# Two transformer blocks on one core: the first norm split by kinds of token, and keys and values moved ahead of the second half of the modulation

## What is computed

```python
def rmsnorm(x, g):
    xf = x.astype(jnp.float32)
    y = xf * lax.rsqrt(jnp.mean(xf * xf, axis=-1, keepdims=True) + EPS)
    return (y * g.astype(jnp.float32)).astype(x.dtype)

def adaln(cvec, w_mod, b_mod):
    m = jax.nn.silu(cvec) @ w_mod + b_mod
    return jnp.split(m, 6, axis=-1)

def modulate(x, g, shift, scale):
    return rmsnorm(x, g) * (1 + scale) + shift

    # in hybrid_layer
    sh1, sc1, gt1, sh2, sc2, gt2 = [m[:, None, :] for m in adaln(c, w_mod, b_mod)]
    csh1, csc1, cgt1, csh2, csc2, cgt2 = adaln(c_ctx, w_mod, b_mod)
    w_q, w_kv, w_gm = split_in_proj(w_in)
    hl = modulate(xl, g_mix, sh1, sc1)
    hc = modulate(xc, g_mix, csh1, csc1)
    kc, vc = keys_values(hc, w_kv, k_gain)
    ql = apply_rope(queries(hl, w_q, q_gain), cos, sin)
    kl, vl = keys_values(hl, w_kv, k_gain)
```

## Time and profile before

| | |
|---|---|
| median of three executions | 1356.51 us |
| the profiled execution, its own time | 1363.62 us |
| span of its trace | 1361.8 us |
| PE / DVE / ACT / POOL busy | 988.6 / 401.5 / 242.9 / 89.8 us |
| share of the span on the chain that ended last | DMA 59%, PE 32%, DVE 7%, ACT 1% |
| `ring<-in_t_w`, the experts' weights, on that chain | 58% |
| mean of the DMA | 354 GB/s |

### The profile page before, as it was taken

How to read it: one execution, slowest core, us unless ns; L and a number is a source line. 1 busy time by engine, 2 the same in 40 slices (tenths; PEclk the granted TensorE clock), 3 DMA queues, 4 the chain that set the end, 5 groups by cost and what they waited for, 6 DMA issues and landing times.

```text
span 1361.8 us, 15239 instructions
## 1 busy us (share of the span) xinstructions
PE 988.6 (73%) x6607; PEld 501.4 (37%) x6607; DVE 401.5 (29%) x950; ACT 242.9 (18%) x489; POOL 89.8 (7%) x127
## 2 busy tenths in 40 slices
PE   5999987567666765566566575666656797999998
PEld 3765833212211111111111111111111386999876
DVE  4767411011011101101011010101101167785685
ACT  3535110000000000000000000000000265653463
POOL 1210000000020000000000000000000054300030
PEclk8999889887887788877788877878778798999999
DMA  9898889999999999999999999999999941344501
GB/s 396 368 391 320 353 347 428 426 428 428 426 429 427 428 428 427 429 428 426 428 427 428 428 428 428 428 428 426 428 428 428 419 152 63 124 161 149 186 1 47
DMA packets 35031, 482.47 MB, mean 354 GB/s; under 512 B 3858, under 2 KB 3860, under 8 KB 5780
## 3 DMA queue, kind: packets, MB, share of 16 engines
q1 hardware_dynamic: 34672, 480.97, 84.3%
q10 hardware_dynamic: 292, 0.53, 0.1%
HBM read 480.43 MB, written 1.05 MB: 354 GB/s over the span
## 4 chain that ended last, share of the span: by engine, by line
DMA 59%; PE 32%; DVE 7%; ACT 1%; issue 1%; POOL 0%; SPq 0%; POOLq 0%; DVEq 0%; ACTq 0%
DMA ring<-in_t_w 58%; PE PS L510 7%; PE PS L1035 5%; PE PS L498 4%; PE PS L1081 2%; PE PS L487 2%; PE PS L702 2%; PE PS L1269 2%; PE PS L805 1%; DVE RR L468 1%; PE PS L1096 1%; DVE S L648 1%; PE PS L827 1%; DMA KC<-in_consts 1%; PE PS L597 1%
## 5 line engine op out<-in xcount | busy, mean ns | idle before, releaser
L1035 PE MATMUL PS<-ring,S 128*32 128x512 f32 x2016 | 317.2, 763 | 207.5 <-DMA ring<-in_t_w 205.0
L1081 PE MATMUL PS<-ring,S 128*32 128x512 f32 x1008 | 174.6, 828 | 103.8 <-DMA ring<-in_t_w 95.7
L1035 PEld LDWEIGHTS PS<-ring,S 128*32 128x32 f32 x2016 | 62.8, 126 | 440.7 <-DMA ring<-in_t_w 320.9
L516 DVE COPY S<-PS 128x512 f32<-128x512 f32 (+2 forms) x47 | 32.0, 683 | 319.3 <-PE PS L1081 294.7
L510 PE MATMUL PS<-SR,RR 128*128 128x256 f32 x736 | 118.3, 284 | 0.0
L1081 PEld LDWEIGHTS PS<-ring,S 128*32 128x32 f32 x1008 | 34.1, 132 | 227.0 <-DMA ring<-in_t_w 148.7
L510 PEld LDWEIGHTS PS<-SR,RR 128*128 128x128 f32 x736 | 105.5, 191 | 1.2 <-issue 0.9
L1617 DVE TENSOR_SCALAR S<-PS,KC 128x256 f32<-128x256 f32 x16 | 7.7, 483 | 282.9 <-PE PS L1065 282.9
L2088 ACT ACTIVATE S<-PS 128x512 f32<-128x512 f32 x16 | 9.6, 597 | 444.7 <-PE PS L1035 444.7
L456 ACT ACTIVATE RR<-ring 128x1024 fp32r<-128x1024 f32 (+2 forms) x91 | 85.5, 1006 | 8.9 <-PE PS L510 8.9
L518 ACT ACTIVATE S<-PS 128x512 f32<-128x512 f32 (+2 forms) x50 | 28.0, 570 | 330.7 <-PE PS L487 329.5
(11 more groups left out here) (312 smaller groups left out, 1007.4 us busy)
## 6 DMA issues: line engine op xcount, KB each, us to landing
ring<-in_t_w SPq DMA_DIRECT2D x189, 2048.0 KB, 36.2
ring<-in_t_mod SPq DMA_DIRECT2D x12, 2048.0 KB, 12.6
ring<-in_t_out SPq DMA_DIRECT2D x6, 2048.0 KB, 7.9
S<-in_t_w SPq DMA_DIRECT2D x3, 2048.0 KB, 13.6
ring<-in_t_e_g SPq DMA_DIRECT2D x2, 2048.0 KB, 12.6
ring<-in_t_o_q SPq DMA_DIRECT2D x2, 2048.0 KB, 7.8
ring<-in_t_o_k SPq DMA_DIRECT2D x2, 2048.0 KB, 8.2
ring<-in_t_o_v SPq DMA_DIRECT2D x2, 2048.0 KB, 7.8
```

What stands on the lines that cost most here:

```text
L516: lane.e.tensor_copy(dst, src).then_inc(*lane.mark(out_of(key), *names))
L1035: m = pe.e.matmul(PS[32 * j:32 * j + 32, b, :], expert_rows(2 * k + kk, e_, e_ + 1), place[name, e_, k][:, kk, 512 * j:512 * j + 512], sta ...
L1081: m = pe.e.matmul(PS[q:q + 32, b, :], HT[e_ % 2][:, 128 * s + 32 * j:128 * s + 32 * j + 32], place["w2", e_, j][:, s, 512 * dh:512 * dh + ...
```

## The change

The norm goes by kinds. POOL makes a constant -0.5 itself and takes it in place of the one in `KC`; it computes the factors for `x` as soon as its two squares are there, and then those for `ctx`. DVE scales `x` before it squares its half of `ctx`. PE's groups of transposes hold two columns of one kind, so that groups 0 to 3 need only `xn` 0 and 1 (and the identity). On PE the two parts of s1 stand later: kv 0 and 1, s1 scale, kv 2, s1 shift, kv 3, columns of s1, kv 4 to 7.

```diff
--- before.py
+++ after.py
@@ -317,7 +317,7 @@
     XN = reg(4096, 2, D)
     junk = reg(12288, D)
     junk2 = reg(8192 + 2048, D)
-    ss1, rs1 = col(4), col(4)
+    ss1, rs1, minus_half = col(4), col(4), col(2)
     RAW = reg(0, 2, 8, 256)
     HI, LO = regr(4096, 2, 8, 256), regr(0, 2, 8, 256)
     HL = (HI[:, 0], LO[:, 0])
@@ -829,21 +829,25 @@
             if ks[-1] == 7:
                 m.then_inc(*pe.mark(("kv", 0), ("kv", 1), ("kv", 2), ("kv", 3), used(("in", "kv"))))
 
-        pe.wait_ge(*[("xn", i) for i in range(4)])
-        for k in range(8):
-            transposes(pe, ("raw", k), ALL6, [(XN if i < 2 else XC)[:, i % 2, 128 * k:128 * k + 128] for i in range(4)])
+        for n in range(8):
+
+            if n % 4 == 0:
+                pe.wait_ge(*[("xn", n // 2 + i) for i in range(2)])
+            transposes(pe, ("raw", n), ALL6, [(XC if n >= 4 else XN)[:, i, 128 * k:128 * k + 128]
+                                              for k in (2 * (n % 4), 2 * (n % 4) + 1) for i in range(2)])
         mod_part("s0", 0)
         mod_part("s0", 1)
         mod_cols("s0")
-        mod_part("s1", 0)
         for i in range(4):
             banks.take(("kv", i), ALL6, hold=True)
             pe.wait_ge(banks.was["kv", i])
         kv_part(range(2))
+        mod_part("s1", 0)
+        kv_part((2,))
         mod_part("s1", 1)
-        kv_part((2,))
+        kv_part((3,))
         mod_cols("s1")
-        kv_part(range(3, 8))
+        kv_part(range(4, 8))
         for i in range(4):
             banks.release(("kv", i))
         for i in range(2):
@@ -1316,18 +1320,23 @@
     def dve_program(dve):
         dve.stage("mix")
         dve.wait_ge(("load", "x"))
-        dve.settle(dve.e.tensor_tensor_reduce(junk2, X[:, 1, :], X[:, 1, :], 1.0 / D, 0.0, ALU.mult, ALU.add, ss1[:, 1:2]))
-        dve.wait_ge(("load", "ctx"))
-        dve.e.tensor_tensor_reduce(junk2, XC[:, 1, :], XC[:, 1, :], 1.0 / D, 0.0, ALU.mult, ALU.add,
-                                   ss1[:, 3:4]).then_inc(*dve.mark("squares dve"))
-        dve.wait_ge("rs1")
-        for i in range(4):
-            src = X[:, i, :] if i < 2 else XC[:, i - 2, :]
-            dst = XN[:, i, :] if i < 2 else XC[:, i - 2, :]
-            dve.e.tensor_scalar(dst, src, rs1[:, i:i + 1], None, ALU.mult).then_inc(*dve.mark(("xn", i)))
-        for k in range(0, 8, 2):
-            dve.wait_ge(("raw", k))
-            copy_out(dve, ("raw", k), RAW[:, :, k, :], PS[:, banks.of["raw", k], :].rearrange("p (r t) -> p r t", r=2))
+        dve.e.tensor_tensor_reduce(junk2, X[:, 1, :], X[:, 1, :], 1.0 / D, 0.0, ALU.mult, ALU.add,
+                                   ss1[:, 1:2]).then_inc(*dve.mark(("squares dve", 0)))
+        for kind in range(2):
+            dve.wait_ge(("rs1", kind))
+            for i in range(2 * kind, 2 * kind + 2):
+                src = X[:, i, :] if i < 2 else XC[:, i - 2, :]
+                dst = XN[:, i, :] if i < 2 else XC[:, i - 2, :]
+                dve.e.tensor_scalar(dst, src, rs1[:, i:i + 1], None, ALU.mult).then_inc(*dve.mark(("xn", i)))
+            if kind == 0:
+                dve.wait_ge(("load", "ctx"), ("squares dve", 0))
+                dve.e.tensor_tensor_reduce(junk2, XC[:, 1, :], XC[:, 1, :], 1.0 / D, 0.0, ALU.mult, ALU.add,
+                                           ss1[:, 3:4]).then_inc(*dve.mark(("squares dve", 1)))
+
+        for n in range(0, 8, 2):
+            dve.wait_ge(("raw", n))
+            j = 2 * (n % 4)
+            copy_out(dve, ("raw", n), RAW[:, n // 4, j:j + 2, :], PS[:, banks.of["raw", n], :].rearrange("p (k t) -> p k t", k=2))
 
         def mod_first(h):
 
@@ -1937,10 +1946,11 @@
     def act_program(act):
         act.stage("mix")
         act.wait_ge(("load", "x"))
-        act.settle(act.e.activation(junk, X[:, 0, :], ACT.Square, scale=float(D) ** -0.5, accum_out=ss1[:, 0:1]))
+        act.settle(act.e.activation(junk, X[:, 0, :], ACT.Square, scale=float(D) ** -0.5, accum_out=ss1[:, 0:1]),
+                   ("squares act", 0))
         act.wait_ge(("load", "ctx"))
         act.e.activation(junk, XC[:, 0, :], ACT.Square, scale=float(D) ** -0.5, accum_out=ss1[:, 2:3]).then_inc(
-            *act.mark("squares act"))
+            *act.mark(("squares act", 1)))
         act.wait_ge(("load", "consts"), "cvec zero")
         for r in range(2):
             act.e.activation(cvec[:, :, 32 + r], RT[:, 8 * r:8 * r + 8], ACT.Silu).then_inc(*act.mark(("cv", r)))
@@ -1949,9 +1959,10 @@
             act.wait_ge(("mod", g), before)
             copy_out(act, ("mod", g), bm[:, ROW_OF[g], :], PS[:, banks.of["mod", g], :])
 
-        for k in range(1, 8, 2):
-            act.wait_ge(("raw", k))
-            copy_out(act, ("raw", k), RAW[:, :, k, :], PS[:, banks.of["raw", k], :].rearrange("p (r t) -> p r t", r=2))
+        for n in range(1, 8, 2):
+            act.wait_ge(("raw", n))
+            j = 2 * (n % 4)
+            copy_out(act, ("raw", n), RAW[:, n // 4, j:j + 2, :], PS[:, banks.of["raw", n], :].rearrange("p (k t) -> p k t", k=2))
         for h in range(2):
             mod_row(f"s{h}")
             if h == 0:
@@ -2236,9 +2247,13 @@
     def pool_program(pool):
         pool.stage("mix")
         pool.e.memset(cvec[:], 0.0).then_inc(*pool.mark("cvec zero"))
-        pool.wait_ge("squares act", "squares dve", ("load", "consts"))
-        rstd(pool, rs1, ss1, "rs1")
-        pool.wait_ge(("xn", 3))
+        pool.settle(pool.e.memset(minus_half, -0.5))
+        for kind in range(2):
+            c = slice(2 * kind, 2 * kind + 2)
+            pool.wait_ge(("squares act", kind), ("squares dve", kind))
+            pool.settle(pool.e.tensor_scalar(rs1[:, c], ss1[:, c], EPS, None, ALU.add))
+            pool.e.tensor_tensor(rs1[:, c], rs1[:, c], minus_half, ALU.pow).then_inc(*pool.mark(("rs1", kind)))
+        pool.wait_ge(("xn", 3), ("load", "consts"))
         for tab, g in ((tabq, qgb), (tabk, kgb)):
             for i, (tr, half) in enumerate(((cosT, 0), (sinT, 1), (sinT, 0), (cosT, 1))):
                 t = pool.e.tensor_tensor(tab[:, i, :, :], tr, bc(g[:, 32 * half:32 * half + 32], [P, 2, 32], 1), ALU.mult)
```

## The result

| | before | changed |
|---|---|---|
| median | 1359.16 us (18 runs, 1356.22 to 1371.77) | 1367.25 us (18 runs, 1364.97 to 1375.86) |
| ratio to before, with its 95% interval | | 1.0052 (1.0033 to 1.0071) |
| profiled execution / its span | 1363.62 / 1361.8 us | 1371.08 / 1369.3 us |
| full stretch of transfers begins | 217.39 us | 221.30 us |

The ratio is worth 7.1 us (4.5 to 9.7) of 1359; forecast were 2.65, and 1359.2 us with a range to 1362.4. The two medians themselves stand 8.1 us apart; the ratio is the figure that is used here. The direction was right, the size was not. The median of before is also 2.65 us higher over 18 runs than over the three that the forecast started from, by chance the same number as the forecast.

The account below looks back on a forecast made before the run. Expert-weight transfers were taken to bound the kernel, their start set by PE's path ahead of 182 us. T +0.35 and second place +2.3 gave +2.65 us on the median 1356.51: 1359.2 us, range 1354.2 to 1362.4.

Parts of the forecast that it names:

- the second fall: Clock falling to half in the wait ahead of kv 4, slowing the 48 matmuls of kv 4 to 7: +2.3 us.
- What bounds the kernel: Landings of expert weights fill the time from 217.39 us; a microsecond PE wins or loses ahead of 182 us reaches the end.
- Part 1: Norm by kinds: PE starts transposes at 10.4 to 10.5 us, ends 4 us earlier; 2.5 left after the s0 shift.
- the shift part ends at 20.15 + 1.82 = 22.0: s0 shift on PE: starts when its unit lands at 20.15 us, runs at full clock, ends at 22.0 instead of 24.54.
- Part 2: kv ahead of s1 on PE: more work ahead of T, half clock at kv 0 costing 2.3 us; T later by 0.35.
- T: End of the s1 shift on PE: 37.17 us before, forecast 37.5; kv 4 begins 5.2 us behind it.
- The second place: Stretch of 3.8 us without full matmuls ahead of kv 4: clock falls, 4.6 us at half clock, cost +2.3 us.
- The queries follow them at once on PE: Behind the 48 matmuls of kv 4 to 7: no wait before the queries, so nothing hides the half clock's cost.
- The base: Profiled execution lies 7.1 us above the median; the forecast difference of 2.65 us is added to the median, 1356.51 us.
- The whole start comes through: Rival: kv 0 begins 4.0 us earlier and all behind it does too, 1352.5 us; chance 0.1.
- The clock holds at one place or at both: Rivals, at kv 0 and kv 4: one fall gives 1356.9 us, chance 0.2; no fall gives 1354.5, chance 0.06.
- More is lost: Rival: both half-clock stretches at their long end, +4 us, and a later stretch falling less well: 1360.5 to 1363; chance 0.09.

Follow-up runs that it names:

- e8: Changed kernel plus dummy transposes in its first waits only (18 ahead of the s0 shift, 5 and 28 around the columns of s0); ratio to before 1.0034.
- e3: Changed kernel plus dummy transposes in four waits (20, 5, 28 and 20); ratio to before 1.0018 (0.9995 to 1.0041).
- e4: Norm by kinds with PE's old order, plus dummy transposes in its waits (20, 5, 16 and 6); ratio to before 0.9998 (0.9976 to 1.0019).
- e7: Changed kernel with the turn of PSUM banks moved on by four behind keys and values; one execution, queries begin at 53.22 us.
- e2: Kernel before with PE's new order alone, norm as before; ratio to before 1.0048 (1.0023 to 1.0072), profiled twice.
- e1: Changed kernel with PE's old order, so the norm by kinds alone; ratio to before 1.0010 (0.9987 to 1.0033).
- e6: Changed kernel plus 20 dummy transposes in its last wait alone, behind the columns of s1; ratio to before 1.0046 (1.0029 to 1.0062).
- e5: Changed kernel with s1 in one piece behind kv 0 and 1, kv 2 to 7 after its columns, dummies in first waits, banks moved on; ratio to before 0.9994.
- e9: Kernel before plus dummy transposes in its first wait alone (5 ahead of the columns of s0, 13 behind); ratio to before 0.9994.

## Why the prediction was right or wrong

The steps that failed are two. The clock in the wait for the s0 shift unit was put at nothing and cost 1.7 us, and the start was taken from a single profile of before that was 1.2 us late. Two smaller terms go with them: the second fall, 0.6 short, and a bank, 0.5.

**What bounds the kernel: right.** The landings of expert weights fill 221.30 to 1080 us as they filled 217.39 to 1076, and over all profiles the start of the queries comes through to them, within the 3 us named above.

**Part 1: right up to one step.** PE turned from 10.39 to 15.5 and waited for the s0 shift unit until 20.18 (forecast 20.15). The step "the shift part ends at 20.15 + 1.82 = 22.0" failed: it ended at 23.8, since the clock fell in that very wait. Of all the waits that the change makes, I asked of two whether the clock survives them and left the first out, so that its cost stood at nothing in the sum. I had its length at 1.4 us and it was 2.73 (the transposes ended some 1.3 sooner than I took). e8 shows the step: with the wait filled, the part takes 1.92 us and kv 0 begins at 27.50, with it open at 29.15. Cost: 1.7 us, the largest error of the sum.

**Part 2: right in mechanism.** T was 39.6, forecast 37.5; take off the late kv 0 and it is 37.7. kv 4 began 5.2 us behind T, as forecast. That the order at full clock puts more on the path than the old one agrees with e3 and e4 in time, and is shown in the rows by e8, whose clock was full up to T: T was 35.9 there, and 34.6 in the third profile of before (32.70 + 1.93), in which the clock never fell.

**The second place: mis-sized.** Forecast +2.3, measured 8.63 - 5.73 = 2.9 in the first profile, and in the four others with this wait left open 2.8 (e7), 1.7 (e8), 1.6 and 0.2 (e2, where the first profile had no fall). The mean of the five is 1.8, under the 2.3; for this profile the term was 0.6 short. I had taken 4.6 us of half clock; from 44.79, where the 48 matmuls begin, to 50.9 it was 6.1.

**Not seen: the bank.** "The queries follow them at once on PE" was wrong by 0.5 us (e7). The order of instructions shows no added wait by name; who had the bank last does.

**The sum.** From the first profile of before: 2.4 at T, 2.9 at the 48 matmuls, 0.5 at the bank, 5.8 of the 6.0 us at the queries, where 2.65 were forecast; 0.2 is the overlap of the queries with kv 7 before. The other 1.1 of the 7.1 us are the base.

**The base: wrong.** "I add the difference to the median" took one profiled execution of before as the typical one. It was 1.2 us later at the queries than the mean of three (47.93 against 46.7). 53.90 - 46.7 = 7.2 us, near to what the ratio says (7.1). With one profile of the one and three of the other, whose times spread by more than 2 us, so close an agreement is luck; e7, the same kernel but for the bank, had 53.22. I had written that the stretch of 3.1 us "was enough for a fall", from one example; of three profiles one had none. The same mistake made the range too narrow: it left 3.2 us above the forecast.

**The rivals.** "The whole start comes through" is refuted by the result, and e1 shows why: even in the old order the norm alone wins nothing that can be measured. "The clock holds at one place or at both" did not happen in the two profiles that have the whole change (its own and e7); in the first profile of e2 it held at the second place. "More is lost" was the case, beyond its own 1363 us, and for reasons of which it names one, the length of the stretches.

**Open.** In the first pair of profiles 6.0 us at the queries were 3.9 at 217 us. The 24 matmuls near 130 us account for 1.6 of the difference; the rest, and the spread behind the last landing, I take for the chance of where half clock falls, and did not test it.

## What to carry to other kernels

When work is started earlier, look up when each transfer behind it lands, and ask of every wait that this opens, the short first one too, what TensorE's clock does in it. A step that is moved forward to fill a gap pushes back what stood there. Find the step with the long tail (here the s1 shift, whose copy, columns and factors take 5 us), add up all that now stands ahead of it, and weigh that against the gap; and keep independent work behind it as cover for the tail. Where the clock rises and falls by chance, one profile is one draw: take two or three of the kernel before, before a difference of 0.2% is worked out from it.

## What the runs showed of the hardware

- Waits of PE of 2.73 and 2.71 us (changed, e7) ended with half clock for about 3.4 us (20.1 to 23.6). Waits of 2.44 and 2.42 us at the same place (e1, e6) were followed by a fall too, at 21.0.
- The stretch ahead of the s1 scale in the kernel before, with four narrow matmuls in it, was 3.1, 3.8 and 3.4 us long in three executions. The clock fell in it or just behind it in the first two, for 6.9 and 3.7 us, and not in the third. The stretch of 3.8 us from the columns of s1 to kv 4 in the new order brought a fall in four of five profiles.
- Dummy transposes of the identity in a wait, 0.12 us each, held the full clock over every wait that they filled, in all six kernels that had them. They cost nothing where they ended before the wait did (the s0 shift began at 20.18 in e8, as without them). Where PE had reached the wait late they delayed the next step by up to 0.9 us.
- In the five kernels with dummies ahead of the s1 shift unit's landing (e3, e4, e5, e8, e9) it landed 29.3 to 29.5 us after its issue, in the nine other profiles, e6 with its dummies further on among them, after 28.0 to 28.2. Why was not tried. PE waited for that unit for 1.23 us in e4, 1.31 in e5 and 0.48 in e9.
- With half clock up to its last 0.5 us a group of 24 matmuls of 128 x 256 took 5.15 us, at full clock 3.07, and a modulation part 3.57 to 3.64 against 1.92.
